# Seven block products in place of eight for the first feed-forward weights of an encoder trunk

## The reference

```
def swiglu(x, w_in, w_out):              # w_in 1024 x 5632, w_out 2816 x 1024
    gate, up = jnp.split(x @ w_in, 2, axis=-1)
    return (jax.nn.silu(gate) * up) @ w_out
x = x + 0.5 * rms_norm(swiglu(rms_norm(x, g[FFN1_PRE]), ffn_w_in[l, 0], ffn_w_out[l, 0]), g[FFN1_POST])
```

## Time and profile before

| | us |
|---|---|
| median of 3 timed runs | 2477.03 (2475.92 to 2477.12) |
| the profiled execution | 2475.8 |
| its span, first to last instruction | 2473.9 |

### The profile page before, as it was taken

How to read it: one execution, slowest core, us unless ns; L and a number is a source line. 1 busy time by engine, 2 the same in 40 slices (tenths; PEclk the granted TensorE clock), 3 DMA queues, 4 the chain that set the end, 5 groups by cost and what they waited for, 6 DMA issues and landing times.

```text
span 2473.9 us, 47010 instructions
## 1 busy us (share of the span) xinstructions
PE 2448.9 (99%) x20196; PEld 2390.3 (97%) x20196; DVE 1021.9 (41%) x1335; ACT 923.2 (37%) x1509; POOL 114.9 (5%) x185
## 2 busy tenths in 40 slices
PE   7999999999999999999999999999999999999998
PEld 7999999998999999999999999999989999999998
DVE  4232227645365443232253332275364655333322
ACT  4333215227453443332253332252274444333312
POOL 0000000420000000000000000006000000000000
PEclk9999999999999999999999999999999999999999
DMA  4333323330234132233232323232302431332322
GB/s 158 94 94 93 103 92 122 86 128 30 69 111 137 43 120 94 93 96 100 77 120 85 102 85 103 86 128 78 139 10 71 143 111 60 103 101 85 102 95 77
DMA packets 66245, 236.39 MB, mean 96 GB/s; under 512 B 8883, under 2 KB 10633, under 8 KB 65601
## 3 DMA queue, kind: packets, MB, share of 16 engines
q1 hardware_dynamic: 57600, 209.74, 26.5%
q0 software_dynamic: 8224, 24.12, 3.0%
q10 hardware_dynamic: 288, 0.59, 0.1%
HBM read 232.29 MB, written 2.12 MB: 95 GB/s over the span
## 4 chain that ended last, share of the span: by engine, by line
PE 97%; ACT 1%; DVE 1%; issue 1%; DMA 0%; SPq 0%; DVEq 0%; ACTq 0%
PE bank L330 26%; PE bank L334 26%; PE bank L332 26%; PE bank L533 3%; PE bank L384 2%; PE bank L386 2%; PE bank L385 2%; PE bank L508 2%; PE bank L604 1%; PE bank L371 1%; PE bank L463 1%; PE bank L486 1%; PE bank L658 1%; PE bank L479 0%; PE bank L546 0%
## 5 line engine op out<-in xcount | busy, mean ns | idle before, releaser
L266 DVE TENSOR_TENSOR wl<-raw,wh 128x1024 fp32r<-128x1024 f32 x392 | 483.5, 1233 | 441.6 <-ACT wh L261 439.9
L330 PE MATMUL bank<-uH,wh 128*128 128x256 f32 x3328 | 662.2, 280 | 0.0
L332 PE MATMUL bank<-uL,wh 128*128 128x256 f32 x3328 | 659.9, 279 | 0.0
L334 PE MATMUL bank<-uH,wl 128*128 128x256 f32 x3328 | 659.7, 279 | 0.0
L261 ACT ACTIVATE wh<-raw 128x1024 fp32r<-128x1024 f32 x392 | 413.0, 1054 | 601.1 <-PE bank L334 519.6
L330 PEld LDWEIGHTS bank<-uH,wh 128*128 128x128 f32 x3328 | 506.5, 188 | 2.4 <-issue 2.2
L334 PEld LDWEIGHTS bank<-uH,wl 128*128 128x128 f32 x3328 | 507.0, 188 | 0.0
L332 PEld LDWEIGHTS bank<-uL,wh 128*128 128x128 f32 x3328 | 506.8, 188 | 0.0
L1079 DVE TENSOR_TENSOR tmp<-bank,tmp 128x512 f32<-128x512 f32 x88 | 60.9, 692 | 623.5 <-PE bank L334 594.7
L330 PE MATMUL bank<-wh,hH 128*128 128x256 f32 x1408 | 281.5, 281 | 0.0
L334 PE MATMUL bank<-wh,hL 128*128 128x256 f32 x1408 | 281.1, 281 | 0.0
(11 more groups left out here) (200 smaller groups left out, 2732.2 us busy)
## 6 DMA issues: line engine op xcount, KB each, us to landing
raw<-in_w_first SPq DMA_DIRECT2D x176, 512.0 KB, 3.6
raw<-in_w_proj SPq DMA_DIRECT2D x128, 512.0 KB, 3.5
raw<-in_w_second SPq DMA_DIRECT2D x88, 512.0 KB, 3.5
gain_rows<-in_grow POOLq DMA_DIRECT2D x15, 512.0 KB, 4.9
strip<-bias_of_distance POOLq DMA_DIRECT2D x2, 2688.0 KB, 12.2
strip<-in_rpb POOLq DMA_DIRECT2D x96, 24.0 KB, 2.2
xs<-in_x SPq DMA_DIRECT2D x4, 512.0 KB, 8.8
fwd<-in_k_fwd POOLq DMA_DIRECT2D x4, 512.0 KB, 4.9
```

The source lines that it names most:

```text
L266: e.tensor_tensor(wl[u % RING][:], raw[u % RAWS][:], wh[u % RING][:].bitcast(F32), ALU.subtract).then_inc(split_ready, 1)
L330: e.matmul(b[:, c], still_h, hi[:, c], start=first and c.start == 0, stop=False)
L332: e.matmul(b[:, c], still_h, lo[:, c], start=False, stop=False)
L334: mm = e.matmul(b[:, c], still_l, hi[:, c], start=False, stop=last and c.stop == n)
```

## The change

Pairs 3 to 22 of each input stage are computed by Strassen's scheme in the form with seven products. The blocks are: the 2 x 2 weights (A: the gate tile's two feature halves, D: the value tile's), and the 2 x 2 input (feature halves x token halves). VectorE forms four sums of weight blocks per pair (`s1_s3`, `s2`, `s4`, 512 columns each, fp32) and, once per feed-forward, four sums of input blocks T1 to T4 (`sums_of_t`), from the plain fp32 input: a copy `uF` of the first 256 tokens, made by ScalarE (`u_plain`), and the PSUM banks that still hold the second half. All are split in high and low as before: A whole, S1 and S2, S3 and S4 as tiles of 1024, half of D. `factor_product` multiplies 4 feature tiles x 3 parts of 256 columns, seven times per group. The results are put together by `p1` (ScalarE) and `u2`, `u4_u3`, `c22`, `c12_c21` (VectorE); then come silu and the hidden product, from SBUF. Pair loads go to two sets of tiles (`pairs_of`), both blocks together, when `low_d` has freed the set. The hidden stays in fp32 (`hid`) and is split in the output stage, in a ring of 4 (`hid_high`, `hid_low`). `distances` comes after the second group, and its subtractions before the last but one group. The other weights, the mixer and the attention are as they were.

```diff
--- before.py
+++ after.py
+GROUPS_IN = FT - 2
+PRODUCTS = 7
+QUARTER = 4 * P
...
+pairs_of = [(raw[0][:], raw[1][:]), (side[:], fact["raw_value"][:])]
...
+            def group(q, it=0):
+                for n in range(2):
+                    e.dma_start(pairs_of[q % 2][n], first(L * 88 + f * 44 + RING + 2 * q + n, it)
+                                ).then_inc(group_landed[q % 2], 16)
+            n0 = (2 * L + f) * GROUPS_IN
+            e.wait_ge(split_ready, base + RING)
+            group(0)
+            e.wait_ge(x_sq, (4 * L + 3 * f) * NT + NT)
+            group(1)
+            with e.Fori(1, GROUPS_IN // 2) as it:
+                for q in range(2):
+                    e.wait_ge(low_d, n0 + q - 1 + 2 * it)
+                    group(q, it)
+            e.wait_ge(low_d, n0 + GROUPS_IN - 1)
...
+    def factor_product(base, slot, bH, bL, to):
+        for k in range(4):
+            w = slice(slot % 2 * QUARTER + k * P, slot % 2 * QUARTER + k * P + P)
+            still_h, still_l = (block_of(t, base, slot // 2)[:, w] for t in (wh, wl))
+            e.matmul(to, still_h, bH[:, k, :], start=k == 0, stop=False)
+            e.matmul(to, still_h, bL[:, k, :], start=False, stop=False)
+            mm = e.matmul(to, still_l, bH[:, k, :], start=False, stop=k == 3)
+        mm.then_inc(factor_done, 1)
+    def group(L, f, q, it=0):
+        F, base = 2 * L + f, L * UNITS + U_IN[f]
+        n = GROUPS_IN * F + q + 2 * it
+        begins = isinstance(it, int) and q == 0
+        lo, hi = slice(0, HALF), slice(HALF, T)
+        if begins:
+            e.wait_ge(h_ready, FT * F + 1)
+        else:
+            e.wait_ge(copied_out, n)
+        e.wait_ge(low_a, n + 1)
+        factor_product(base, 0, uH[:, 0:4, lo], uL[:, 0:4, lo], bank[0][:, lo])
+        if not begins:
+            e.wait_ge(c11_ready, n)
+        factor_product(base, 1, uH[:, 4:8, lo], uL[:, 4:8, lo], bank[1][:, lo])
+        e.wait_ge(low_s12, n + 1)
+        if begins:
+            e.wait_ge(t_split, 4 * F + 1)
+        factor_product(base, 2, fact["T2H"], fact["T2L"], bank[1][:, hi])
+        if begins:
+            e.wait_ge(h_ready, FT * F + 2)
+            e.wait_ge(t_split, 4 * F + 2)
+        else:
+            e.wait_ge(c22_ready, n)
+        factor_product(base, 3, fact["T1H"], fact["T1L"], bank[2][:, lo])
+        e.wait_ge(low_s34, n + 1)
+        if begins:
+            e.wait_ge(t_split, 4 * F + 3)
+        factor_product(base, 4, fact["T3H"], fact["T3L"], bank[2][:, hi])
+        if not begins:
+            e.wait_ge(c_ready, n)
+        factor_product(base, 5, uH[:, 4:8, hi], uL[:, 4:8, hi], bank[3][:, lo])
+        e.wait_ge(low_d, n + 1)
+        if begins:
+            e.wait_ge(t_split, 4 * F + 4)
+        factor_product(base, 6, fact["T4H"], fact["T4L"], bank[3][:, hi])
...
+        first_units(base, 4 * L + 3 * f)
+        group(L, f, 0)
+        group(L, f, 1)
+        if L == f == 0:
+            distances()
+        with e.Fori(1, GROUPS_IN // 2) as it:
+            for q in range(2):
+                group(L, f, q, it)
+        if L == f == 0:
+            e.wait_ge(s_t5b, 2)
...
+    def u_plain(b, i):
+        if b % 4 in (0, 3):
+            e.wait_ge(u_ready, b * NT + i + 1)
+            e.activation(columns_of(uF, i), by_k(pair[i][:]), ACT.Copy).then_inc(uf_ready, 1)
...
+        def slot_free(q, it, unit, product):
+            if isinstance(it, int) and q + 2 * it == 0:
+                wait_unit(e, base + unit)
+            else:
+                e.wait_ge(factor_done, products_before(F, q - 1, it) + product)
+        def high_of_a(q, it=0):
+            e.wait_ge(group_landed[q % 2], 32 * (GROUPS_IN // 2 * F + q // 2 + 1) + 32 * it)
+            slot_free(q, it, 0, 2)
+            e.activation(block_of(wh, base, 0)[:], pairs_of[q % 2][0], ACT.Copy).then_inc(high_a, 1)
...
+        def p1(q, it=0):
+            e.wait_ge(factor_done, products_before(F, q, it) + 1)
+            if not (isinstance(it, int) and q + 2 * it == 0):
+                e.wait_ge(c11_ready, GROUPS_IN * F + q + 2 * it)
+            e.activation(p1_out, bank[0][:, 0:HALF], ACT.Copy).then_inc(copied_out, 1)
+        def gate_of_group(q, it=0):
+            e.wait_ge(c_ready, GROUPS_IN * F + q + 1 + 2 * it)
+            c = sums[q % 2][:, 0:T]
+            e.activation(c, c, ACT.Silu).then_inc(gate_out, 1)
+        def group(q, it=0):
+            high_of_a(q + 1, it)
+            high_of_s12(q + 1, it)
+            high_of_s34(q + 1, it)
+            gate_of_group(q, it)
+            high_of_d(q + 1, it)
+            p1(q + 1, it)
+        def hid_high(j):
+            e.wait_ge(h_ready, pairs + j + 1)
+            if j >= RING:
+                wait_unit(e, u0 + j - RING)
+            else:
+                e.wait_ge(factor_done, products_before(F, GROUPS_IN - 1) + (3 if j < 2 else 4))
+            e.activation(hs[:, j % RING, 0, :], hid[:, j * T:j * T + T], ACT.Copy).then_inc(hidh_ready, 1)
+        def out_high(j):
+            e.wait_ge(factor_done, products_before(F, GROUPS_IN - 1) + (2, 4, 6, 7)[j])
+            high(e, u0 + j)
+        high_of_t(2, 4)
+        high_of_t(1, 2)
+        gate_of_unit(0)
+        high_of_a(0)
+        high_of_t(3, 5)
+        high_of_t(4, 6)
+        gate_of_unit(1)
+        high_of_s12(0)
+        high_of_s34(0)
+        high_of_d(0)
+        p1(0)
+        group(0)
+        group(1)
+        with e.Fori(1, GROUPS_IN // 2 - 1) as it:
             for q in range(2):
-                n = pairs + q + 1 + 2 * it
-                e.wait_ge(unit_done, base + 2 * q + 1 + RING * it)
-                e.activation(tmp[q][:], bank[2 * q][:], ACT.Silu).then_inc(gate_out, 1)
-                high(e, base + RING + 2 * q, it)
-                e.wait_ge(h_ready, n)
-                e.activation(hH[:, bass.ds((2 * it + q) * T, T)], tmp[2 + q][:], ACT.Copy).then_inc(hidh_ready, 1)
-                high(e, base + RING + 2 * q + 1, it)
+                group(q, it)
+        group(GROUPS_IN - 2)
+        q = GROUPS_IN - 1
+        out_high(0)
+        hid_high(0)
+        out_high(1)
+        hid_high(1)
+        out_high(2)
+        gate_of_group(q)
         load_log_exp()
-        for j in range(FT - RING):
-            high(e, L * UNITS + U_OUT[f] + RING + j)
+        hid_high(2)
+        out_high(3)
+        hid_high(3)
+        for j in range(RING, FT):
+            high(e, u0 + j)
+            hid_high(j)
...
+        def sums_of_t():
+            T1, T2 = plain["T1"], plain["T2"]
+            e.wait_ge(uf_ready, 2 * F + 2)
+            for a in range(2):
+                e.tensor_tensor(T1[:, :, a * P:a * P + P], by_k(pair[2 + a][:])[:, 0:4, :],
+                                uF[:, 0:4, a * P:a * P + P], ALU.subtract).then_inc(t_sum, 1)
+            for a in range(2):
+                e.wait_ge(t_sum, 6 * F + a + 1)
+                e.tensor_tensor(T2[:, :, a * P:a * P + P], by_k(pair[2 + a][:])[:, 4:8, :],
+                                T1[:, :, a * P:a * P + P], ALU.subtract).then_inc(t_sum, 1)
+            e.wait_ge(t_sum, 6 * F + 4)
+            e.tensor_tensor(plain["T3"][:], T2[:], uF[:, 0:4, :], ALU.subtract).then_inc(t_sum, 1)
+            e.tensor_tensor(plain["T4"][:], uF[:, 4:8, :], T2[:], ALU.subtract).then_inc(t_sum, 1)
...
+        def s1_s3(q, it=0):
+            a, d = pairs_of[q % 2]
+            if not (isinstance(it, int) and q == 0):
+                e.wait_ge(low_s12, GROUPS_IN * F + q + 2 * it)
+                e.wait_ge(low_s34, GROUPS_IN * F + q + 2 * it)
+            e.wait_ge(group_landed[q % 2], 32 * (GROUPS_IN // 2 * F + q // 2 + 1) + 32 * it)
+            e.tensor_tensor(S[:, QUARTER:D], d[:, 0:QUARTER], d[:, QUARTER:D], ALU.add).then_inc(s_sum, 1)
+            e.tensor_tensor(S[:, D:D + QUARTER], a[:, 0:QUARTER], d[:, 0:QUARTER],
+                            ALU.subtract).then_inc(s_sum, 1)
...
+        def low_of(n, cols, source, high_done, low_done, q, it):
+            e.wait_ge(high_done, GROUPS_IN * F + q + 1 + 2 * it)
+            e.tensor_tensor(block_of(wl, base, n)[:, 0:cols], source,
+                            block_of(wh, base, n)[:, 0:cols].bitcast(F32), ALU.subtract).then_inc(low_done, 1)
...
+        def u2(q, it=0):
+            e.wait_ge(copied_out, GROUPS_IN * F + q + 1 + 2 * it)
+            e.wait_ge(factor_done, products_before(F, q, it) + 3)
+            e.wait_ge(h_ready, pairs + 2 if isinstance(it, int) and q == 0 else pairs + q + 1 + 2 * it)
+            e.tensor_tensor(in_two(sums[q % 2][:, 0:T]), in_two(bank[1][:]),
+                            p1_out.unsqueeze(1).to_broadcast([P, 2, HALF]), ALU.add).then_inc(c11_ready, 1)
+        def u4_u3(q, it=0):
+            e.wait_ge(c11_ready, GROUPS_IN * F + q + 1 + 2 * it)
+            e.wait_ge(factor_done, products_before(F, q, it) + 5)
+            if not (isinstance(it, int) and q == 0):
+                e.wait_ge(c_ready, GROUPS_IN * F + q + 2 * it)
+            e.tensor_tensor(in_two(u43), in_two(bank[2][:]),
```

(80 more changed lines are left out.)

## The result

| | before | after |
|---|---|---|
| median, us (4 runs each) | 2477.07 (2475.92 to 2481.65) | 2366.65 (2364.76 to 2368.02) |
| the profiled execution, its span | 2475.8, 2473.9 | 2367.66, 2365.8 |

The ratio is 0.955 (95% interval 0.954 to 0.956): faster by 110 us. 2368 was forecast.

What follows compares the result with a forecast made beforehand. The loop was taken to be bound by TensorE's number of matmuls alone. 2475.8 - 112.0 for 960 matmuls + 4 x (0.4 + 0.4) for starts and ends gave 2367.0, forecast as 2368 us, range 2360 to 2405.

Steps and rivals of the forecast that it cites:

- The price of a matmul: Feed-forward input loop: TensorE keeps 116.7 ns per matmul, so 960 fewer save 112.0 us; a group takes 9.80 us.
- VectorE's sum: VectorE's instructions per group, counted by distances of starts, take 9.34 us, under TensorE's 9.80 by 0.46.
- The order: Order of steps within a group: VectorE's and ScalarE's results come before TensorE needs them; price 0.
- Loads: Weight loads in the groups: 1 MB per 9.8 us, asked for early enough; price 0, bound 6 us.
- Start of each feed-forward: Copies by ScalarE and T sums on VectorE before the first groups: worked out as 0, 0.4 us taken per feed-forward.
- End: Last hidden product before the first output unit's second half: margin 0.2 us, 0.4 us taken per feed-forward.
- The sum: Whole program: 2475.8 - 112.0 + 4 x (0.4 + 0.4) = 2367.0 us for the profiled execution; 2368 forecast.
- Rival B: VectorE becomes the loop's bound: whole durations count, 10.35 us per group, 2420 us in all; chance 0.20.
- Rivals C and D: C: each VectorE wait costs 0.10 us, 2514, chance 0.04; D: 0.05 us gap per TensorE product, 2396, chance 0.06.

Runs made afterwards that it cites:

- m96: The changed kernel with the first of the seven products issued twice, 96 matmuls per group again: 2477.24 us, ratio 1.000 to the kernel before.
- v512: The changed kernel with one more VectorE addition of 512 columns at the end of each group's list, into an idle tile: 2372.74 us.
- k3: The changed kernel with one of four feature tiles left out of each of the seven products, 63 matmuls per group instead of 84: 2327.16 us.
- v1024: The changed kernel with two more VectorE additions of 512 columns at the end of each group's list, into idle tiles: 2417.94 us.
- again: The changed kernel run once more, with nothing altered: 2365.22 us.

## Why the prediction was right, step by step

- **The price of a matmul, 116.7 ns, and 112.0 us for 960.** Right: 9.80 us per group, and m96 gives all back. By the Trainium skill (TensorE: Matmul & The Clock Gate, section Back-to-back issue gap) an isolated matmul of 256 columns takes an estimated 109 ns, which would have made 105 us. The measured 116.7 decides.
- **VectorE's sum, 9.34 us.** 9.27 measured (v512 without its addition, k3). The changed kernel shows it too, where VectorE catches up after the start of a feed-forward: c12_c21 at 1227.66, 1236.93, 1246.20 and 1255.47. The term was right in kind; where nothing in front has waited, starts are 0.60 apart, not 0.61. The wait of about 0.5 was 0.47 at c12_c21 (0.38 of it listed as idle) and 0.05 at u2.
- **The order, price 0.** Right: in the loop TensorE waits for nothing. VectorE waits for it at c12_c21 and, which was overlooked, at u2: the worked-out start of u2, 14.3, is just when the third product of the next group ends, 9.8 + 4.2 + 0.3. It did no harm, as VectorE has room. One premise was wrong without harm: the table load of 1.28 us doesn't come once an iteration any more. The changed kernel has four before its silu steps, one per feed-forward, where the kernel before had 44.
- **Loads, price 0.** Right; in the loop neither engine waits for a block.
- **Start of each feed-forward, 0.4 us taken.** The sum was right, the place not. Low A of group 0 was worked out to start 9.5 us after the T sums may begin; the rows (31.62 for the first of them, 41.08 for low A) have 9.46, and no gap follows. But `u_plain`, costed at 0 because it "stands ahead of work that waits for TensorE anyway", cost about 0.5 us at three boundaries: what waits behind it is a square, and VectorE's list behind that, not only the uH copy that I had looked at. The slack of such a step is the smallest along the whole chain to uL, over all three engines.
- **End, 0.4 us taken.** Too much; TensorE's loads are 0.19 us apart at that point instead of 0.12, so it cost 0.07 at most. But this end is where a slower VectorE is paid for first (v512).
- **The sum.** 2475.8 - 112.0 = 2363.8; the profiled execution had 2367.66, 3.9 more. 1.5 are the three boundaries, 0.2 the ends, 1.9 the longer distance of matmuls in one feed-forward (below). 0.3 is left. The 3.2 that I had added for starts and ends is thus 1.5 too much, and that the profiled execution came within 0.7 of the 2367.0 worked out for it is luck: the 1.9 stood in no term. Against the median, 2366.65, the forecast of 2368 is 1.3 too high.
- **Rival B** was the only close one, and the experiments give its condition: 0.53 us per group in the loop, 0.50 with starts and ends. A change with two more sums of 512 columns would have lost half of the gain (v1024: 53 of 110 us). This is also what the hidden's low part (0.69 us, 0.60 from start to start), had it stayed in the loop, would have done by v512: 7.7 us. That is argued from v512, not tried.
- **Rivals C and D**: excluded by k3 and m96.

## What to carry to other kernels

Before trading matmuls for elementwise work, add up the distances of starts on the receiving engine, not its durations: 0.60 and 0.69 us for the same instruction decide here whether the loop is bound by TensorE or by VectorE. Then probe the margin with dummy instructions of two sizes; the one that is free and the one that isn't bracket it, and they show whether the next such change will pay. Look at the end of the stage as well: a small lag per iteration is first paid there. A step that is "hidden" needs every engine behind it looked at: a copy on an idle ScalarE reached TensorE through VectorE's list.

## What the hardware showed beside this

- A VectorE addition or subtraction in fp32 that waits for nothing starts 0.34, 0.60 or 1.13 us after the one before, of 256, 512 or 1024 columns (listed with 0.42, 0.68 and 1.22). That is 0.07 us and 1.04 ns per column. Waits that are already met cost nothing that shows: u2, with three ahead of it, starts 0.60 us after the one before in all 76 lists of v512. One that waits for its direct predecessor starts 0.04 after that one's end. By the Trainium skill (VectorE: DVE Perf Modes, section The DRAIN you can't avoid) the next instruction does not start until the pipe is empty, but the same section adds that a next instruction which is not held back starts earlier. The trace agrees with the latter: 0.60 us from start to start for a listed 0.68. So the section as a whole doesn't speak for rival B, as the prediction had it.
- The distance of TensorE's matmuls has more than one value for the same code. In one feed-forward of the changed kernel's profiled execution c12_c21 came every 9.89 us, not 9.80, with a granted clock of 1.00 over that stretch (866 to 1064) and VectorE waiting 0.35 for TensorE:

```profile
995.53 0.69 DVE L1401 TENSOR_TENSOR tmp<-bank,tmp 128x512 f32<-128x512 f32 x1 [0.35 <-PE bank L501]
1005.42 0.69 DVE L1401 TENSOR_TENSOR tmp<-bank,tmp 128x512 f32<-128x512 f32 x1 [0.35 <-PE bank L501]
```

  In the same kernel's other profiled execution (again) the same place has 9.80:

```profile
994.00 0.69 DVE L1401 TENSOR_TENSOR tmp<-bank,tmp 128x512 f32<-128x512 f32 x1 [0.29 <-PE bank L501]
1003.80 0.69 DVE L1401 TENSOR_TENSOR tmp<-bank,tmp 128x512 f32<-128x512 f32 x1 [0.29 <-PE bank L501]
```

  So it isn't bound to a place in the program. 117.8 instead of 116.7 ns over a feed-forward's 1680 matmuls are 1.9 us, over half the scatter of the timed runs (2364.8 to 2368.0). The output stage has 118.3 in the kernel before, and in the changed one too (the 1056 loads of its first output stage span 124.75 us). Why is open.
